# Both long-convolution filters beside the up panels, start-up loads in another order, and modulation panels summed four to a bank

## The chip, the cores and the metric

One core of a Trainium2 chip runs the whole program. The metric is the device time of one execution in microseconds (us). The kernel before took 2073.51 us (median of 3 runs, 2073.36 to 2076.2).

## What is computed

One transformer block of a first model and two layers of a second, for 256 tokens of width 1024, in float32. What matters here is how the first block begins:

```
h  = x + grid_pos_embed(256);  hc = ctx
m  = split(silu(c)     @ mod_w + mod_b, 9)      # 9 vectors of 1024, for the tokens
mc = split(silu(c_ctx) @ mod_w + mod_b, 9)      # and 9 for the context
h  = half_ffn(h,  m[0],  m[1],  m[2],  w_gate, w_up, w_down)
hc = half_ffn(hc, mc[0], mc[1], mc[2], w_gate, w_up, w_down)
...                                             # later: modulate(rms_norm(h), m[3], m[4]) and so on
hyena_kernels(256, w1, b1, freq1, w2, b2, freq2, w3)   # two filters ("orders") for a long convolution
```

`half_ffn` takes the RMS norm of its input, scales and shifts it by the first two vectors, multiplies by the gate and up weights (1024 x 2816 each), applies silu, and multiplies by the down weight. The filters come from a small network with two sine layers on position features. They need nothing of x, and are used only much later, in the mixer.

## The kernel before, in words

**Weights.** Every large weight is cut into panels of 128 x 2048 float32 (1 MB). SyncE (SP) issues their loads in order into a ring of four slots, `landing` (L519, L527). GpSimd (POOL) rounds a panel to its high part `whi` (`high`, L569 and L570), VectorE (DVE) subtracts it to get the low part `wlo` (`low`, L643), and TensorE (PE) makes each product of three matmuls: high x high, high x low, low x high (`product`, L1830 to L1832). A panel of the up stage is 48 matmuls with 512 columns, tokens and context side by side.

**Modulation.** The first 8 panels of the stream (`lead`) hold mod_w for the first two of the nine vectors, which the norm of the first half_ffn needs. The other 28 (`rest`) are worked beside the 22 up panels and come through two more slots in `ws` (`load_rest`, L536). One panel is 8 matmuls with `cst`, silu of c and c_ctx, as a stationary of 32 columns, whose first two count (`mod_product`, L1956); the results lie in four groups of 32 partitions. ScalarE (ACT) copies the bank to `mrow` (`mod_copy`, L1512), PE sums the four groups and turns the row into columns with two matmuls against the 0/1 matrix `fold` (`turn`, L1987), and after each four panels DVE adds the bias into `mcol` (`add_mod`, L792). So there are 36 copies, 36 turns and 9 additions.

**Filters.** `filter_layer` (PE, L1997), `sine_argument` (DVE, L745 to L750) and `sine` (ACT, L1502) give the features `h2`. Per order, `taps` (PE, L2010) makes the taps in two halves, `windowed` (DVE, L757) multiplies by the window, `fold_kernel` (L762 to L765) adds and subtracts the two directions, `absolute` (L773 to L775) and `tap_sums` (PE, L2020) give the L1 norm, `inverse_norm` (L779, L781) its reciprocal, `spectrum` (PE, L2034 and L2038) the Fourier transform in four parts, `normed_spectrum` (L788) scales it, and `spill` (ACT, L1498) stores it to HBM.

**The order of the work** is written out by hand, one program per engine, with semaphores between them; each engine runs its list in order, so a wait holds up all behind it. PE's start is: lead 0, lead 1, filter_layer 0, turn 0, lead 2, turn 1, filter_layer 1, lead 3, turn 2, lead 4, turn 3, taps(0, 0), lead 5, turn 4, taps(0, 1), the sums of squares of the tokens (`norm_sum`, L1925), lead 6, turn 5, the sums of squares of the context, lead 7, turns 6 and 7. Then come the 22 up panels, with tap_sums(0) behind panel 0, spectrum(0) behind 1, the taps of order 1 behind 2 and 3, tap_sums(1) behind 5 and spectrum(1) behind 6. From panel 7 on, one rest panel is worked in the middle of an up panel and one behind it, each with the turn of an earlier one but for the first two; two turns stand in the middle of the last up panel.

ACT begins with 14 DMA issues (L1475 to L1489), then makes silu(c) (L1493, semaphore `c_silu`), on which all of PE waits. DVE begins with the two sine arguments, adds the position embedding to h (L805), waits for the window and the folded transform matrix (`hw_in`, two loads), does windowed(0, 0), windowed(0, 1) and fold_kernel(0), then add_mod(0) and add_mod(1), the gains (L816), and the norm: for each of eight chunks k two multiplications (L822), ACT's addition of the shift (L1538) and two subtractions (L828). `low` of the first up panel stands behind the step k == 1.

Of the kernel before, what the change touches and what calls it, by code (L numbers as in the profile page):

```python
# [20 lines left out]
ALU = mybir.AluOpType  # L21
# [49 lines left out]
REST_FROM = 7  # L71
# [15 lines left out]
def columns(*sizes):  # L87
    out, at = {}, 0
    for name, n in sizes:
# [11 lines left out]
                      ("rot_ret", P), ("fold", 2))  # L101
# [6 lines left out]
def shape_constants():  # L108
# [5 lines left out]
    mats["fold"][p % 32 == 0, 0] = 1  # L114
    mats["fold"][p % 32 == 1, 1] = 1
# [111 lines left out]
def build(nc, stream, xT, ctxT, vec1, vec2, lbrow, hyw, mats, tabs, masks, posemb, hyc, window, zT, spectra, out):  # L227
    with ExitStack() as ctx:
# [19 lines left out]
        cst = sb("cst", [P, KD, 32])  # L248
# [49 lines left out]
        mrow = W(2048, UNROLL, COLS)  # L298
# [27 lines left out]
        flb = sb("flb", [P, 4])  # L326
# [90 lines left out]
        flb_in, h3w_in, hw_in = sem("flb_in"), sem("h3w_in"), sem("hw_in")  # L417
        def turn_bank(i):
            return 5 if i == 1 else 4
# [96 lines left out]
        def _(sp):  # L516
            sp.dma_start(v1[:], vec1).then_inc(vec_in, 16)
            for g in range(SLOTS):
                sp.dma_start(landing[:, g], stream[g]).then_inc(landed[g], 16)  # L519
# [17 lines left out]

            for g in range(SLOTS, N_LEAD + REST_FROM + SLOTS):
# [5 lines left out]
            follow = N_LEAD + REST_FROM + SLOTS + N_REST // 2  # L544
# [79 lines left out]
        def _(dve):  # L624
# [127 lines left out]
            def windowed(o, u):  # L752
                dve.wait_ge(h3_mm, 2 * o + u + 1)
                if o and u == 0:
                    dve.wait_ge(kf_mm, 4)
                for d in range(2):
                    last = v.tensor_tensor(kern[:, d, u * 512:(u + 1) * 512], ps[:, 6 + d], hwindow[:, d, u], ALU.mult)  # L757
                last.then_inc(win_mul, 1)
# [31 lines left out]
            def add_mod(i):  # L790
                dve.wait_ge(mod_turned, i * UNROLL + UNROLL)
                v.tensor_tensor(mcol[:, i * 8:i * 8 + 8, :],  # L792
                                ps[:, turn_bank(i), 0:16].rearrange("p (c b) -> p c b", b=2),
                                m1("mod_b", 0, 72)[:, i * 8:i * 8 + 8].unsqueeze(2).to_broadcast([P, 8, 2]), ALU.add
                                ).then_inc(mod_added, 1)
# [3 lines left out]
            sine_argument(1)  # L799
# [19 lines left out]
            for k in range(KD + 1):  # L819
# [11 lines left out]
                if k == 1:  # L831
                    low(G_UP1, G_UP1 % SLOTS)

            def beside_up1(i):
                if i == 0:
                    absolute(0)
                if i == 5:
                    absolute(1)
                if i == 1:
                    inverse_norm(0)  # L840
                if i == 2:
                    normed_spectrum(0, 0)
                    normed_spectrum(0, 1)
                if i == 3:
                    normed_spectrum(0, 2)
                    normed_spectrum(0, 3)
                    windowed(1, 0)
                if i == 4:
                    windowed(1, 1)
                    fold_kernel(1)  # L850
                if i == 6:
                    inverse_norm(1)
                if i == 7:
                    normed_spectrum(1, 0)
                    normed_spectrum(1, 1)
                if i == 8:
                    normed_spectrum(1, 2)
                    normed_spectrum(1, 3)
                q = i - REST_FROM - 3
                if q >= 0 and q % 2 == 0:  # L860
# [1655 lines left out]
```

## Time and profile before

| | |
|---|---|
| median of 3 runs | 2073.51 us |
| the profiled execution | 2071.93 us, its span 2069.9 us |
| PE busy | 1932.9 us (93%) |
| DVE, POOL, ACT busy | 1147.3, 601.3, 383.9 us |
| granted TensorE clock, mean | 0.976 |
| moved by DMA | 307.83 MB, mean 149 GB/s |

Times in the trace count from the span's start. A row of the timeline gives start, duration, engine, line, what is written and read, how many instructions were merged, and in brackets how long the engine stood idle before and what released it. PE is the matmul, PEld its weight load; ACTq and SPq are DMA issues of ScalarE and SyncE. The granted clock is 1.0 at 2.4 GHz and 0.5 at 1.2 GHz. Each float32 matmul leaves more than one record, so a modulation panel of 8 matmuls is "x16" and a turn of 2 is "x4".

### The profile page before, as it was taken

The numbers are of one execution on the slowest core, as the hardware profiler recorded it, in microseconds if no ns is written. First come the engines' busy times: TensorE is split into PE (matmuls) and PEld (weight loads), VectorE is DVE, ScalarE is ACT, GpSimd is POOL, SyncE is SP. The second block draws the span as 40 slices with busy tenths as digits, with TensorE's granted clock in tenths as the row PEclk, the third lists the DMA queues.
The fourth block names the chain that finished last, engine by engine and source line by source line (L and its number), as shares of the span: only waits on it lengthen the run. The fifth ranks groups of instructions, "written<-read, shape, count | busy, mean of one in ns | idle before, by whom it ended". The sixth has DMA issues, their size and how long they took to land.

```text
span 2069.9 us, 33025 instructions
## 1 busy us (share of the span) xinstructions
PE 1932.9 (93%) x13818; PEld 1758.2 (85%) x13818; DVE 1147.3 (55%) x1219; ACT 383.9 (19%) x718; POOL 601.3 (29%) x505
## 2 busy tenths in 40 slices
PE   4899999999997878899989999889999999889999
PEld 2576777887997867799989997789999999689999
DVE  3652221325258976644575776675556676576554
ACT  1200000113122230211122122411112102432110
POOL 0111111121235611233333332133334333123333
PEclk8899999999999989999999999999999999999999
DMA  8336655321233212355544443235554434134552
GB/s 311 113 108 218 237 210 201 131 102 61 103 127 128 95 69 102 112 188 183 181 152 166 143 143 122 102 126 184 182 183 175 151 140 156 69 141 165 183 183 102
DMA packets 44913, 307.83 MB, mean 149 GB/s; under 512 B 5376, under 2 KB 5888, under 8 KB 8320
## 3 DMA queue, kind: packets, MB, share of 16 engines
q1 hardware_dynamic: 40752, 292.66, 39.8%
q10 hardware_dynamic: 4048, 13.49, 1.8%
q8 instruction: 93, 1.52, 0.3%
q14 instruction: 20, 0.16, 0.0%
HBM read 302.98 MB, written 3.15 MB: 148 GB/s over the span
## 4 chain that ended last, share of the span: by engine, by line
PE 78%; DVE 12%; issue 4%; POOL 2%; ACT 2%; DMA 2%; ACTq 0%; DVEq 0%; POOLq 0%
PE ps L1830 23%; PE ps L1831 22%; PE ps L1832 22%; DVE wlo L643 3%; POOL whi L570 2%; DMA ws<-in_hyc 2%; PE ps L1956 1%; PE ps L2312 1%; PE ps L1925 1%; PE ps L2219 1%; PE ps L2336 1%; DVE xlo L703 1%; PE ps L1987 1%; PE ps L2179 1%; PE ps L2289 1%
## 5 line engine op out<-in xcount | busy, mean ns | idle before, releaser
L1830 PE MATMUL ps<-xhi,whi 128*128 128x256 f32 (+1 forms) x3680 | 1121.0, 305 | 37.5 <-DVE xlo L651 21.4
L1831 PE MATMUL ps<-xlo,whi 128*128 128x256 f32 (+1 forms) x3680 | 1104.1, 300 | 0.0
L1832 PE MATMUL ps<-xhi,wlo 128*128 128x256 f32 (+1 forms) x3680 | 1103.6, 300 | 0.0
L643 DVE TENSOR_TENSOR wlo<-landing,whi 128x2048 fp32r<-128x2048 f32 x242 | 562.3, 2323 | 460.0 <-POOL whi L570 459.3
L1830 PEld LDWEIGHTS ps<-xhi,whi 128*128 128x128 f32 x3680 | 710.1, 193 | 74.2 <-issue 31.1
L1831 PEld LDWEIGHTS ps<-xlo,whi 128*128 128x128 f32 x3680 | 710.3, 193 | 22.8 <-issue 2.2
L1832 PEld LDWEIGHTS ps<-xhi,wlo 128*128 128x128 f32 x3680 | 709.6, 193 | 21.2
L569 POOL TENSOR_TENSOR whi<-landing,ones 128x128 fp32r<-128x128 f32 x242 | 124.4, 514 | 1445.1 <-PE ps L1832 1404.2
L570 POOL TENSOR_SCALAR whi<-landing 128x1920 fp32r<-128x1920 f32 x242 | 442.9, 1830 | 0.0
L881 DVE TENSOR_TENSOR big<-big,ps 128x512 f32<-128x512 f32 x22 | 15.1, 687 | 184.7 <-ACT big L1555 184.7
L1467 ACT ACTIVATE xhi<-big 128x512 fp32r (+3 forms) x66 | 45.9, 696 | 385.7 <-PE ps L1832 331.2
L1830 PE MATMUL ps<-whi,xhi 128*128 128x256 f32 (+1 forms) x288 | 84.9, 295 | 10.4 <-DVE wlo L643 4.0
L1831 PE MATMUL ps<-wlo,xhi 128*128 128x256 f32 (+1 forms) x288 | 82.4, 286 | 0.0
L1832 PE MATMUL ps<-whi,xlo 128*128 128x256 f32 (+1 forms) x288 | 82.2, 285 | 0.0
L651 DVE TENSOR_TENSOR xlo<-big,xhi 128x512 fp32r<-128x512 f32 (+1 forms) x82 | 62.0, 756 | 13.9 <-ACT xhi L1777 13.7
L1830 PEld LDWEIGHTS ps<-whi,xhi 128*128 128x128 f32 x288 | 56.4, 196 | 13.4 <-DVE wlo L643 5.0
L1831 PEld LDWEIGHTS ps<-wlo,xhi 128*128 128x128 f32 x288 | 56.5, 196 | 0.0
L1832 PEld LDWEIGHTS ps<-whi,xlo 128*128 128x128 f32 x288 | 56.4, 196 | 0.0
L1196 DVE TENSOR_REDUCE smx<-ps 128x2 f32<-128x512 f32 x32 | 22.1, 690 | 52.2 <-PE ps L2312 52.2
L1731 ACT ACTIVATE ws<-ps,smx 128x256 f32<-128x256 f32 x64 | 29.7, 470 | 110.4 <-DVE smx L1198 110.4
L2179 PE MATMUL ps<-ws 128*128 128x128 f32 x224 | 30.8, 298 | 16.2 <-DVE ws L978 16.1
L1809 ACT ACTIVATE big<-ws 128x512 f32 (+1 forms) x32 | 20.2, 632 | 137.7 <-DVE ws L1329 137.7
(269 smaller groups left out, 1379.3 us busy)
## 6 DMA issues: line engine op xcount, KB each, us to landing
landing<-in_stream SPq DMA_DIRECT2D x250, 1024.0 KB, 4.8
ws<-in_stream SPq DMA_DIRECT2D x28, 1024.0 KB, 4.8
spectra<-big ACTq DMA_DIRECT2D x8, 256.0 KB, 6.1
ws<-spectra ACTq DMA_DIRECT2D x2, 1024.0 KB, 4.9
ws<-in_tabs ACTq DMA_DIRECT2D x1, 1280.0 KB, 5.5
h<-in_xT ACTq DMA_DIRECT2D x1, 1024.0 KB, 15.7
ws<-in_window ACTq DMA_DIRECT2D x1, 1024.0 KB, 23.7
ws<-in_ctxT ACTq DMA_DIRECT2D x1, 1024.0 KB, 28.2
```

Of the source, the lines that this page charges most:

```text
L569: pool.tensor_tensor(hi[:, 0:P], panel[:, 0:P], ones[:], ALU.mult)
L570: pool.tensor_scalar(hi[:, P:n], panel[:, P:n], 1.0, 0.0, ALU.mult, ALU.add).then_inc(hi_done, 1)
L643: v.tensor_tensor(wlo[:, s % 2], landing[:, s], whi[:, s % 2].bitcast(F32), ALU.subtract).then_inc(lo_done, 1)
L651: v.tensor_tensor(alo[:, r_phase % 2, :, 0:t], src, ahi[:, r_phase % 2, :, 0:t].bitcast(F32), ALU.subtract).then_inc(act_lo, 1)
L703: v.scalar_tensor_tensor(xlo[:, k, 0:T], h[:, k], gain(k), xhi[:, k, 0:T].bitcast(F32), ALU.mult, ALU.subtract).then_inc(norm_lo, 1)
L1196: lstep(v.tensor_reduce(st[:, 0:2], ps[:, 2 + 2 * (n % 2):4 + 2 * (n % 2), 0:T], AX, ALU.max, negate=True))
L1467: a.activation(ahi[:, j, :, 0:t], src(i + skip), ACT.Identity).then_inc(act_hi, 1)
L1731: last = a.activation(ew[n % 2][:, m], ps[:, 2 + 2 * (n % 2) + m, 0:T], ACT.Exp, bias=st[:, 2 + m:3 + m], scale=0.125, accum_out=st[:, 4 + ...
L1830: mm(out, w_hi, x_hi, start=first, stop=False, skip_group_check=True)
L1831: mm(out, w_hi, x_lo, start=False, stop=False, skip_group_check=True)
L1832: return mm(out, w_lo, x_hi, start=False, stop=last, skip_group_check=True)
L2179: last = mm(ps[:, b + u, o], e[:, x], e[:, x], start=True, stop=True)
```

## The change

Five edits.

1. ACT's first loads: mats, x, the position embedding, the two halves of hyw, zT; then silu(c); then ctx, the window, and the two parts of hw3. The folded transform matrix (with a semaphore of its own) and v2all are issued behind sine(1). The two small loads of `flb` go to SP, between v1 and the first panel.
2. `cst` becomes 6 columns wider, with silu(c) at columns 6 and 7. The stationary of panel j of a group of four starts at column 6 - 2j, so the panel's results land on rows 2j and 2j + 1 of each group of 32 partitions, and four panels add up in one bank. One copy and one turn with 8 columns then do four panels: 9 copies and 9 turns in all.
3. Taps, window and fold of order 0 leave the start. Order o now has both halves of the taps behind panel 4o, window and fold on DVE at 4o + 1, the absolute values at 4o + 2 with tap_sums and three spectrum parts behind that panel, the norm and two scaled parts at 4o + 3 with the last spectrum part behind it, and the other two scaled parts at 4o + 4.
4. The rest panels start behind up panel 7 rather than in the middle of it; the last one stands in the middle of the last up panel, and the last turn behind the seventh of its eight chunks.
5. PE's start: lead 0, 1, filter_layer 0, lead 2, 3, filter_layer 1, lead 4, turn 0, lead 5, tokens' squares, lead 6, context's squares, lead 7, turn 1. DVE adds the embedding before the second sine argument. ACT: sine(0), squares of tokens, sine(1), two loads, squares of context, mod_copy(0), the table load, both roots, mod_copy(1). `low` of the first up panel stands behind k == 2.

```diff
-REST_FROM = 7
+REST_FROM = 8
...
@@ sync
             sp.dma_start(v1[:], vec1).then_inc(vec_in, 16)
+            for d in range(2):
+                sp.dma_start(flb[64 * d:64 * d + 64], vec1[0:64, VEC1["b1"][0]:VEC1["b1"][0] + 4]).then_inc(flb_in, 16)
             for g in range(SLOTS):
                 sp.dma_start(landing[:, g], stream[g]).then_inc(landed[g], 16)
...
-            for i in range(N_REST // 2):
-                load(N_LEAD + REST_FROM + SLOTS + i, (N_LEAD + REST_FROM + SLOTS + i) % SLOTS)
-                load_rest(2 * i)
-                load_rest(2 * i + 1)
+            first_rest = N_LEAD + REST_FROM + SLOTS
+            for g in range(SLOTS, first_rest):
                 load(g, g % SLOTS)
+                if g == first_rest - 2:
+                    load_rest(0)
+            load_rest(1)
+            for i in range(N_REST // 2 - 1):
+                load(first_rest + i, (first_rest + i) % SLOTS)
+                load_rest(2 * i + 2)
+                load_rest(2 * i + 3)
@@ vector
             sine_argument(0)
-            sine_argument(1)
             dve.wait_ge(x_in, 32)
...
-            dve.wait_ge(h_set, 4)
-            dve.wait_ge(hw_in, 32)
-            windowed(0, 0)
-            windowed(0, 1)
-            fold_kernel(0)
+            sine_argument(1)
             add_mod(0)
             add_mod(1)
...
-                if k == 1:
+                if k == 2:
                     low(G_UP1, G_UP1 % SLOTS)
 
             def beside_up1(i):
...
+                o, t = divmod(i, 4)
+                if o < 2 and t == 1:
+                    windowed(o, 0)
+                    windowed(o, 1)
+                    fold_kernel(o)
+                if o < 2 and t == 2:
+                    absolute(o)
+                if o < 2 and t == 3:
+                    inverse_norm(o)
+                    normed_spectrum(o, 0)
+                    normed_spectrum(o, 1)
+                if o in (1, 2) and t == 0:
+                    normed_spectrum(o - 1, 2)
+                    normed_spectrum(o - 1, 3)
+                if i in MOD_TURN:
+                    add_mod(LEAD_GROUPS + MOD_TURN.index(i))
@@ scalar
+            act.dma_start(mat[:], mats).then_inc(small_in, 16)
+            act.dma_start(h[:].rearrange("p k t -> p (k t)"), xT).then_inc(x_in, 16)
+            act.dma_start(ws[:, FILT + 3968:FILT + 3968 + POS], posemb).then_inc(x_in, 16)
             act.dma_start(hyin[0:64, 0:128], hyw[:, 0:128]).then_inc(hy_in, 16)
             act.dma_start(hyin[64:128, 0:128], hyw[:, 0:128]).then_inc(hy_in, 16)
             act.dma_start(zfeat, zT).then_inc(hy_in, 16)
...
+            a.activation(cst[:, :, C_AT:C_AT + 2], m1("c", 0, 2 * KD).rearrange("p (k b) -> p k b", b=2), ACT.Silu
+                         ).then_inc(c_silu, 1)
+            act.dma_start(ws[:, 0:2048], ctxT).then_inc(ctx_in, 16)
+            act.dma_start(hwindow.rearrange("p d u c -> p (d u c)"), window).then_inc(hw_in, 16)
...
+            sine(1)
+            act.dma_start(fdft, hyc[:, 1024:1792]).then_inc(dft_folded_in, 16)
+            act.dma_start(v2all[:], vec2.rearrange("l p n -> p l n")).then_inc(v2all_in, 16)
             act.wait_ge(ctx_in, 16)
             for b in range(4):
                 squares(1, hc, b)
-            mod_copy(7)
+            mod_copy(0)
             log_exp()
             norm_rms(0, 2)
             norm_rms(1, 3)
+            mod_copy(1)
@@ tensor
+            def mod_product(n, panel):
+                i, j = divmod(n, UNROLL)
+                at_ = C_AT - 2 * j
                 for k in range(KD):
                     q = 32 * (k % 4)
-                    last = mm(out[q:q + 32], cst[:, k], panel[:, k * COLS:(k + 1) * COLS], start=k < 4, stop=k >= 4,
+                    last = mm(ps[q:q + 32, mod_bank(i), 0:COLS], cst[:, k, at_:at_ + 32], panel[:, k * COLS:(k + 1) * COLS],
+                              start=j == 0 and k < 4, stop=j == UNROLL - 1 and k >= 4, skip_group_check=True)
...
             lead(0)
             lead(1)
             filter_layer(0)
+            lead(2)
+            lead(3)
+            filter_layer(1)
+            lead(4)
             turn(0)
...
-                elif 0 <= j < N_REST:
+                elif i >= REST_FROM:
                     feature_panel(s, up_out(i), 0, 2 * T, (0,))
                     rest(j)
-                    if j:
-                        turn(N_LEAD + j - 2)
                     last = feature_panel(s, up_out(i), 0, 2 * T, (1,))
...
+                if i >= REST_FROM - 1 and j + 1 < N_REST - 1:
                     rest(j + 1)
-                    if j:
-                        turn(N_LEAD + j - 1)
+                if i in MOD_COPY[:-1]:
+                    turn(LEAD_GROUPS + MOD_COPY.index(i))
+                o, t = divmod(i, 4)
+                if o < 2 and t == 0:
+                    taps(o, 0)
+                    taps(o, 1)
+                if o < 2 and t == 2:
+                    tap_sums(o)
+                    spectrum(o, (0, 1, 2))
+                if o < 2 and t == 3:
+                    spectrum(o, (3,))
```

`MOD_COPY` is 9, 11, ..., 21 and `MOD_TURN` 10, 12, ..., 20, 21: ACT copies a group in the second half of an odd up panel, PE turns it behind that panel, and DVE adds it in the next even one. `load_rest(0)` still waits for window (1, 1), `load_rest(1)` for the last spectrum part of order 1, and the later ones for the rest panel two before.

## Rows read from the trace of the kernel before

**Rows 1.** Busy time, share of the DMA engines and GB/s of one stretch:

```profile
core 0: us, PE busy (x) PEld busy (x) DVE busy (x) ACT busy (x) POOL busy (x), PEclk, DMA share, GB/s
30.00:40.00 10.00, 0.00 (x0) 0.00 (x0) 0.56 (x1) 0.00 (x0) 0.00 (x0) 0.57 1.02 418
```

**Rows 2.** The chain that ended last, start-up (start us, us, what):

```profile
8.23 31.13 DMA ws<-in_hyc
```

**Rows 3.** Timeline of the start, DMA issues of ScalarE:

```profile
2.00 0.60 ACTq L1477 DMA_DIRECT2D big<-in_zT  x1
6.72 0.45 ACTq L1485 DMA_DIRECT2D ws<-in_posemb  x1
7.69 0.51 ACTq L1487 DMA_DIRECT2D ws<-in_ctxT  x1
8.72 2.52 ACTq L1489 DMA_DIRECT2D v2all<-in_vec  x1
```

**Rows 4.** DMA issues by line: KB each, us from issue to landing:

```profile
ws<-in_ctxT ACTq DMA_DIRECT2D x1, 1024.0 KB, 28.2
...
ws<-in_posemb ACTq DMA_DIRECT2D x1, 136.0 KB, 17.9
big<-in_zT ACTq DMA_DIRECT2D x1, 128.0 KB, 8.3
```

**Rows 5.** Timeline of the start, compute of 12 to 29 us:

```profile
12.89 3.64 PE L1956 MATMUL ps<-landing,cst 128*32 128x256 f32 x32 [12.89 <-ACT cst L1493]
...
16.46 1.12 PE L1997 MATMUL ps<-big,ws 64*64 64x256 f32 x4
...
17.69 0.55 DVE L745 TENSOR_SCALAR big<-ps,flb 128x256 f32<-128x256 f32 x1 [16.24 <-PE ps L1997]
...
20.63 0.42 ACT L1502 ACTIVATE ws<-big 128x256 f32<-128x256 f32 x1 [3.65 <-DVE big L750]
...
25.09 2.77 DVE L805 TENSOR_TENSOR h<-h,ws 128x256 f32<-128x256 f32 x8
...
26.18 2.34 ACT L1386 ACTIVATE big<-h 128x512 f32<-128x512 f32 x4
```

**Rows 6.** Timeline, from the sums of squares to the norm:

```profile
42.79 4.78 PE L1925 MATMUL ps<-big,ones 128*128 128x256 f32 x16
...
49.59 3.72 PE L1925 MATMUL ps<-big,ones 128*128 128x256 f32 x16 [0.48 <-ACT big L1386]
...
53.24 1.07 PE L1956 MATMUL ps<-landing,cst 128*32 128x256 f32 x16
...
55.67 0.25 DVE L816 TENSOR_SCALAR gains<-mcol 128x8 f32<-128x8 f32 x2
...
57.93 0.48 DVE L822 SCALAR_TENSOR_TENSOR big<-h,gains,rstd 128x256 f32<-128x256 f32 x1 [2.01 <-ACT rstd L1382]
```

**Rows 7.** The chain, one step of the norm:

```profile
63.38 0.79 DVE xlo L828 x2
```

**Rows 8.** Timeline, the first up matmul and the first tap sums:

```profile
62.65 0.80 PE L1830 MATMUL ps<-xhi,whi 128*128 128x512 f32 x1 [7.22 <-DVE wlo L643]
...
78.94 3.66 PE L2020 MATMUL ps<-ws,ones 128*128 128x512 f32 x4 [2.22 <-DVE ws L775]
```

**Rows 9.** The chain, filter work between the up panels:

```profile
110.28 1.06 PE ps L2010 x4
...
145.53 1.72 PE ps L2020 x4
```

**Rows 10.** The chain, three rest panels in turn:

```profile
176.20 1.00 PE ps L1956 x16
...
182.90 1.00 PE ps L1956 x16
...
190.03 1.00 PE ps L1956 x16
```

**Rows 11.** Timeline of DVE in up panel 5, the end of the absolute values:

```profile
141.71 1.22 DVE L775 SCALAR_TENSOR_TENSOR ws<-ws,big 128x1024 f32<-128x1024 f32 x1
```

**Rows 12.** Line of the rest loads, all 28, us to landing:

```profile
DMA to landing us min/median/max: 4.7/4.8/8.7
```

More of the change, by code:

```diff
@@ L70 @@
 PANELS = G_LAYER + LAYERS * PER_LAYER
-REST_FROM = 7
+REST_FROM = 8
+N_GROUP, LEAD_GROUPS = N_MOD // UNROLL, N_LEAD // UNROLL
+C_AT = 2 * (UNROLL - 1)
 DVE_LINKS, ACT_LINKS = 65, 6
@@ L113, in shape_constants @@
     mats["ident"][:] = np.eye(P)
-    mats["fold"][p % 32 == 0, 0] = 1
-    mats["fold"][p % 32 == 1, 1] = 1
+    for r in range(2 * UNROLL):
+        mats["fold"][p % 32 == r, r] = 1
     mats["block64"][:] = (p[:, None] // 64 == p[None] // 64)
@@ L325, in build @@
         ang = chunks(33, 2)
-        flb = sb("flb", [P, 4])
+        flb = scol[:, 0:4]
         KF_BANK = (6, 7, 4, 5)
@@ L753, in windowed @@
                 dve.wait_ge(h3_mm, 2 * o + u + 1)
+                if o == 0 and u == 0:
+                    dve.wait_ge(hw_in, 16)
                 if o and u == 0:
@@ L1893, in last_panel @@
                         beside()
+                    if k == KD - 2:
+                        behind()
                 return last
@@ L2004, in taps @@
                 elif u == 0:
-                    pe.wait_ge(kf_done, 2)
-                else:
-                    pe.wait_ge(win_mul, 2 * o + 1)
+                    pe.wait_ge(kf_done, 4)
+                if o == 0 and u == 1:
+                    pe.wait_ge(mod_added, 3)
                 for d in range(2):
                     r = slice(64 * d, 64 * d + 64)
-                    last = mm(ps[:, 6 + d], h2[r, u * P:(u + 1) * P], hw3[r, o * 512:(o + 1) * 512], start=True, stop=True)
+                    last = mm(ps[:, KF_BANK[2 * u + d]], h2[r, u * P:(u + 1) * P], hw3[r, o * 512:(o + 1) * 512], start=True, stop=True)
                 last.then_inc(h3_mm, 1)
@@ L2021, in tap_sums, with spectrum @@
                 last.then_inc(l1_mm, 1)
-            def spectrum(o):
-                for m in range(4):
+            def spectrum(o, ms):
+                for m in ms:
                     if m == 0:
-                        pe.wait_ge(win_mul, 2 * o + 2)
-                        pe.wait_ge(mod_added, 3)
+                        pe.wait_ge(folded_k, o + 1)
+                        if o == 0:
+                            pe.wait_ge(dft_folded_in, 16)
                     if m == 3:
@@ L2043, in _ @@
             filter_layer(0)
+            lead(2)
+            lead(3)
+            filter_layer(1)
+            lead(4)
             turn(0)
-            lead(2)
-            turn(1)
-            filter_layer(1)
-            lead(3)
-            turn(2)
-            lead(4)
-            turn(3)
-            taps(0, 0)
             lead(5)
-            turn(4)
-            taps(0, 1)
             pe.wait_ge(const_set, 3)
@@ L2059, in _ @@
             lead(6)
-            turn(5)
             for b in range(4):
@@ L2063, in _ @@
             lead(7)
-            turn(6)
-            turn(7)
+            turn(1)
             def up_out(i):
```

179 lines of the change are left out of this document (58 added, 121 removed).

## The prediction

> **What bounds the kernel now.** I read the busy table by stretches first. After the start-up TensorE is busy nearly all the time and everything it does adds to the time, so a gain has to come from PE work left out of the up stage, or from a first up matmul that starts earlier. Before that the table shows a hole: from 30 to 40 us PE does nothing, while the DMA engines are full, moving 418 GB/s [rows 1]. The chain of waits names what the hole waits for: the folded transform matrix, issued at 8.23 and there 31.13 us later, at 39.4 [rows 2]. DVE waits for it before it windows the taps of order 0, PE waits for DVE before the second half of those taps, and the sums of squares, leads 6 and 7 and the norm stand behind in PE's list. The timeline gives the rest: PE's first matmul at 12.89, released by silu(c), which stands behind 14 DMA issues of ACT; the first filter layer at 16.46, though its last load, zT, was there at 2.00 + 8.3 = 10.3 [rows 3 to 5]; the norm's first multiplication at 57.93; the first up matmul at 62.65 [rows 6, 8]. In the up stage I read the chain of waits for the spacing of like work.
>
> **Up stage: turns.** A rest panel without a turn is 182.90 - 176.20 = 6.70 us from the next, with one 190.03 - 182.90 = 7.13 [rows 10]; a turn costs 0.43 on PE, which is the bound there. Of 28 turns 7 stay: 21 x 0.43 = 9.0 us saved. The four panels summed in a bank cost what they did: the same matmuls with the same 32 columns. A turn with 8 columns instead of 2 moves six columns more in each of two matmuls; I take it at the same 0.43. ACT's copy leaves nothing on the path: it stands half an up panel before its turn. The last one, behind four of the last panel's eight chunks, has two chunks and more before its turn.
>
> **Up stage: filters.** Today tap_sums(0) is waited for by 2.22 us and takes 3.66, where the same work in the full-clock stretch takes 1.72 without a wait [rows 8, 9]: 2.22 + 3.66 - 1.72 = 4.2 saved, since DVE now has all of panel 2 for the absolute values. Against that both halves of the taps of order 0 come in, 2 x 1.06 = 2.1 [rows 9]. Spectra and order 1 are the same work at other places. Do they wait? In today's panel 5 DVE ends the absolute values at 141.71 + 1.22 = 142.9 and PE asks for them at 145.53 [rows 9, 11]: 2.6 us of slack, in the very pattern that both orders now get. Window and fold in one panel are one pair of multiplications more than today in a panel that has two taps before it; I take nothing. Net of the filters: 4.2 - 2.1 = 2.1.
>
> **Up stage: queues.** On SP, load_rest(1) now waits for the last spectrum part of order 1, and a panel load and load_rest(2) queue behind it. It lands 4.7 to 8.7 us after its issue [rows 12], and PE wants it after half a panel, 6.70 less the rest product's 1.00 and its edges, about 5.5 [rows 10]. So nothing at the median, at most 3.2 once. The loads behind it are wanted some panels later. Every later rest load has a whole period of 13.6 (2 x 6.70 and, every second time, a turn) less one rest product, 12.4: no wait at 8.7.
>
> **Start-up, up to the first filter layer.** silu(c) comes behind six issues instead of 14, so leads 0 and 1 run as their panels land; the two small flb loads hold up SP's first panel by about 1.3 us (two issues like zT's 0.60), which the next wait hides. That wait is zT. It now stands behind mats, x (1024 KB) and the embedding (136 KB), in a queue that shares full DMA engines with SP's panels. Lower bound by bytes: mats, x and embedding are 1.61 MB, at 418 GB/s 3.9 us, so 10.3 + 3.9 = 14.2. Upper bound: the embedding's landing today, 6.72 + 17.9 = 24.6 [rows 3, 4], behind all that will be ahead of zT and the two parts of hw3 besides. I take 19.0: the upper bound less two more small transfers, at 2.8 each as a guess inside the bounds. The layer takes 1.2 (16.46 to 17.69) [rows 5], so DVE starts at 20.3 rather than 17.69.
>
> The Trainium skill speaks against this part: "DMA: Bandwidth & Descriptors", section Queues, rings and completion order, says that each DMA engine takes packets in turn from the queues that have work, so a small transfer behind others pays for its place rather than its size. The trace agrees: zT, 128 KB, took 8.3 us [rows 4]. By this rule as an estimate each of the three transfers put ahead drags a 1 MB panel along, which gives zT at about 21.5, and the sum below would be 2.5 us worse.
>
> **Start-up, from there to the norm.** PE has turn(0) ahead of lead 5, and turn(0) waits for a copy that ACT makes behind the squares of the context. So the path is: sine argument 2.94 (17.69 to 20.63), additions 2.77, second sine argument 2.94, sine 0.42 [rows 5]; two DMA issues, 0.5 and 2.52 as v2all's today [rows 3]; squares 2.34 [rows 5]; copy and turn 1.2 (the 2.68 from 53.24 to 55.92 less lead 7's 1.07, the gains' 0.25 and the short bias addition); lead 5, 1.5 between 1.07 and twice that, since PE has stood idle and its clock is low then (0.57 granted in the hole); token sums 4.78, lead 6 1.07, context sums 3.72, and from lead 7 to the gains 2.68 less a turn, 2.25 [rows 1, 6]. The roots and their table load are now hidden behind lead 7. That is 28.9, with 0.8 for a dozen handovers 29.7. The norm starts at 20.3 + 29.7 = 50.0, so 7.9 earlier. The context, at 35.9 today (7.69 + 28.2) [rows 3, 4], has less ahead of it and should land near 25, before ACT asks at 32.
>
> **Low behind k == 2.** One norm step is two multiplications and two subtractions, 2 x 0.79 = 1.6 [rows 7]. The first up matmul comes 1.6 later in the norm, and PE, not DVE, sets the pace of panel 0 today, so 1.6 is lost. It would cost less if DVE's steps set that pace.
>
> **Sum.** 9.0 + 2.1 + 7.9 - 1.6 = 17.4 us. The profiled execution took 2071.93 (span 2069.9), so its like would be 2054.5; the median of the runs stands 1.6 above it, at 2073.51, and gives 2056.1.
>
> **Rivals.**
> (a) The filter's loads are early: zT by the lower bound, 14.2, and v2all's issue costs 0.5 (today it is the last of a full row of issues). The norm starts at 15.5 + 27.7 = 43.2, 14.7 earlier; in all 9.0 + 2.1 + 14.7 - 1.6 = 24.2, so 2049.3. For it: 128 KB is little. Against: rows 4.
> (b) The start-up gives nothing back: the one turn that gates five PE items, a cold clock through both sums, zT at 24.6, and the norm starts at 56 to 58. Then the up stage alone counts: 9.0 + 2.1 - 1.6 = 9.5 and up to 2 more, 2062 to 2064. For it: every small load waits its turn today. Against: the 10 us hole has no successor in the new lists.
> (c) The turn saves less than 0.43, say because eight columns cost, or DVE is late at window and fold: half of 9.0 gone, 2060.6.
> (d) Slower: the rest loads set the pace. Each of two slots goes load, product, load; a period of 13.6 leaves 12.4 for a load. At 17.9 us, which the embedding took when the DMA engines were full [rows 4], 13 periods would be 5.5 longer each, 72 in all: 2128. It decides from a landing of 13.7 (13 x 1.3 = 17). Against: none of 28 took over 8.7 [rows 12], and the order of loads is nearly today's.
> (e) That four panels in a bank are not one copy and one turn: the lists say so plainly, and no wait undoes it.
>
> **Chances.** The forecast 0.55, (a) 0.20, (b) 0.13, (c) 0.08, (d) 0.02, and 0.02 for a disturbance that I do not see. The likeliest is 2056.1. From (a) and (b) I take the range 2049.5 to 2063.5: it drops the outer half of (a) and the end of (b), and (d). A measurement of this kernel tells 0.2%, 4.1 us, from no change: faster by over that 0.94, within it 0.03, slower 0.03.
>
> **What would show it.** PE's first matmul near 8; the first filter layer between 15 and 24, and right at 19; a wait of turn(0) for ACT's copy, with leads and sums close behind it; the norm near 50, the first up matmul 6.3 behind it. Panel 0 runs into the taps without a wait. Spacing of rest panels 6.70, with a turn every fourth, 7 turns behind the lead groups. From the end of panel 0 to the last up matmul 11 us less than today. It is wrong if the norm starts after 56, if PE waits at a tap_sums or at rest 1, or if the copy stands on the path in the up stage.

## The result, and the profile after

The changed kernel took 2049.73 us (median of 4 runs, 2048.82 to 2050.41) where the kernel before took 2073.51 (4 runs, 2073.36 to 2076.2): a ratio of 0.9883 [0.9868, 0.9899], 24 us less. The forecast was 2056.1, so the kernel came out 6.4 us below the forecast, at the lower end of its range (2049.5 to 2063.5). The profiled executions (2071.93 and 2049.11) stand 1.6 and 0.6 us below their medians, and their spans differ by 2069.9 - 2047.1 = 22.8 us. I divide up these 22.8; the forecast of the same quantity was 17.4.

The busy table by stretches, same columns as [rows 1]; the fourth column group is DVE, the last two numbers are the DMA engines' share and GB/s:

```profile
30.00:40.00 10.00, 8.34 (x53) 5.58 (x54) 0.17 (x1) 3.78 (x7) 0.00 (x0) 0.70 1.02 395
...
52.49:56.40 3.91, 3.91 (x9) 3.13 (x10) 3.91 (x11) 2.19 (x5) 0.00 (x0) 0.50 0.75 245
...
65.47:351.62 286.15, 286.15 (x1540) 208.04 (x1540) 96.83 (x84) 16.22 (x29) 46.84 (x42) 1.00 0.51 191
```

The hole of [rows 1] is gone: 8.34 of 10 us busy. The last line is the up stage from the end of panel 0 to the last up matmul: PE is busy for all of its 286.15 us, at a granted clock of 1.00, so none of the new waits stands on the path there. The same stretch of the kernel before:

```profile
62.65:68.80 6.15, 6.15 (x15) 4.80 (x16) 6.15 (x16) 3.63 (x8) 0.00 (x0) 0.50 0.51 173
...
76.72:374.56 297.84, 295.62 (x1617) 217.22 (x1616) 88.95 (x75) 24.32 (x50) 48.09 (x42) 0.99 0.53 183
```

The 22.8 us come from three places, each bounded by the same two events in both kernels:

| stretch | before | after | less | forecast |
|---|---|---|---|---|
| start to the norm's first multiplication | 57.93 | 46.19 | 11.7 | 7.9 |
| from there to the first up matmul | 4.72 | 6.30 | -1.6 | -1.6 |
| panel 0, first matmul to the last | 14.07 | 12.98 | 1.1 | 0 |
| end of panel 0 to the last up matmul | 297.84 | 286.15 | 11.7 | 11.1 |
| the rest of the span | 1695.3 | 1695.5 | -0.2 | 0 |

So two thirds of the 5.4 us by which the forecast of the span fell short lie in the start-up. This is its chain of waits (start, length, what), to be set against [rows 2, 5, 6]:

```profile
4.37 17.89 DMA landing<-in_stream
22.31 1.93 PE ps L1947 x16
...
25.34 0.55 DVE big L760
...
28.28 0.34 ACT ws L1498
28.66 0.45 ACTq L1514
29.15 2.19 ACT big L1386 x4
...
31.66 1.02 PE ps L1978 x4
32.68 1.87 PE ps L1947 x16
34.55 4.35 PE ps L1914 x16
38.89 1.00 PE ps L1947 x16
39.89 3.65 PE ps L1914 x16
43.55 1.04 PE ps L1947 x16
...
46.19 1.67 DVE big L835 x4
```

Its long wait is the landing of a panel, for lead 3 at 22.31 (L1947 is lead, L1988 filter_layer, L1914 the sums of squares, L1978 turn). Nothing in it is the folded matrix, and nothing is zT. The timeline shows how zT dropped out:

```profile
3.50 0.64 ACTq L1480 DMA_DIRECT2D big<-in_zT  x1
...
10.88 1.93 PE L1947 MATMUL ps<-landing,cst 128*32 128x256 f32 x16 [10.88 <-DMA landing<-in_stream]
...
15.31 1.11 PE L1988 MATMUL ps<-big,ws 64*64 64x256 f32 x4
...
22.31 1.93 PE L1947 MATMUL ps<-landing,cst 128*32 128x256 f32 x16 [3.03 <-DMA landing<-in_stream]
```

silu(c) now ends at 5.7, yet PE's first matmul waits for its panel until 10.88 (forecast near 8); lead 1 waits likewise, and the first filter layer comes right behind lead 1 without a wait. zT had landed at 3.50 + 11.3 = 14.8.

In the up stage the spacing of rest panels is as [rows 10]: 6.70 without a turn and 7.13 with one, now only every fourth time.

```profile
181.19 1.00 PE ps L1947 x16
...
187.90 1.00 PE ps L1947 x16
188.90 0.54 PE ps L1978 x4
...
195.03 1.00 PE ps L1947 x16
```

The taps and the tap sums, which the forecast priced from [rows 9]:

```profile
65.47 1.92 PE ps L2001 x8
...
89.37 1.72 PE ps L2008 x4
...
118.78 1.92 PE ps L2001 x8
```

Both halves of the taps took 1.92 instead of 2 x 1.06, in order 1 (118.78) as in order 0, and the tap sums 1.72 without a wait, as forecast.

### The profile page after: what moved, and what is told of

The parts are those of the page before. It is cut to its first block, busy times and chain, and to the rows that moved or that the text cites. A ratio compares the mean times of both kernels' runs of the same rounds, so it can differ in the third digit from the quotient of the medians.

```text
span 2047.1 us, 32753 instructions
## 1 busy us (share of the span) xinstructions
PE 1918.0 (94%) x13710; PEld 1744.7 (85%) x13710; DVE 1146.0 (56%) x1219; ACT 374.5 (18%) x691; POOL 600.6 (29%) x505
## 4 chain that ended last, share of the span: by engine, by line
PE 80%; DVE 11%; issue 4%; POOL 2%; ACT 2%; DMA 1%; SPq 0%; ACTq 0%; DVEq 0%; POOLq 0%
PE ps L1817 24%; PE ps L1818 23%; PE ps L1819 23%; DVE wlo L658 2%; POOL whi L585 2%; PE ps L1947 2%; PE ps L2290 1%; DMA landing<-in_stream 1%; PE ps L2197 1%; PE ps L1914 1%; PE ps L2314 1%; DVE xlo L718 1%; PE ps L2157 1%; PE ps L2267 1%; DVE ws L978 1%
## 5 line engine op out<-in xcount | busy, mean ns | idle before, releaser
L1818 PEld LDWEIGHTS ps<-xlo,whi 128*128 128x128 f32 x3680 | 710.1, 193 | 21.7 <-issue 1.4
L1817 PE MATMUL ps<-whi,xhi 128*128 128x256 f32 (+1 forms) x288 | 84.9, 295 | 10.5 <-DVE wlo L658 4.0
L1544 ACT ACTIVATE big<-ps 128x512 f32<-128x512 f32 x22 | 13.2, 598 | 224.1 <-PE ps L1819 224.1
```

The costliest lines, as they stand in the source:

```text
L1817: mm(out, w_hi, x_hi, start=first, stop=False, skip_group_check=True)
L1818: mm(out, w_hi, x_lo, start=False, stop=False, skip_group_check=True)
```

## The experiments

Twelve kernels ran in three batches, each beside the kernel before. Ratios are to that kernel in the same batch, with a 95% interval; the medians of before were 2073.19, 2071.92 and 2071.42 us.

| kernel | batch | median us | ratio |
|---|---|---|---|
| a_low_k1 | 1 | 2047.43 | 0.9874 [0.9853, 0.9895] |
| b_filter1_early | 1 | 2050.78 | 0.9889 [0.9867, 0.9911] |
| c_turn0_late | 1 | 2049.56 | 0.9880 [0.9859, 0.9902] |
| d_combined | 1 | 2047.78 | 0.9875 [0.9857, 0.9893] |
| e_spare_turns | 2 | 2060.43 | 0.9938 [0.9922, 0.9955] |
| f_before_fdft_apart | 2 | 2063.51 | 0.9959 [0.9946, 0.9971] |
| g_filter_loads_first | 2 | 2048.79 | 0.9881 [0.9863, 0.9899] |
| h_v2all_in_burst | 2 | 2048.60 | 0.9886 [0.9868, 0.9904] |
| i_flb_on_act | 3 | 2051.78 | 0.9897 [0.9874, 0.9921] |
| j_high_after_low | 3 | 2049.23 | 0.9883 [0.9866, 0.9900] |
| k_window_late | 3 | 2043.58 | 0.9852 [0.9833, 0.9871] |
| l_window_late_high | 3 | 2043.15 | 0.9856 [0.9838, 0.9874] |

The changed kernel ran four times; i ran twice, d five times, f seven and the others four. The intervals are 5 to 10 us wide, so differences of 1 to 3 us are read from the traces, by the times of like events.

### The turns: e_spare_turns

The 21 turns that the change removes are put back as spare ones, behind rest panels, with nothing that waits for them.

```diff
+            def spare_turn():
+                for c in range(2):
+                    mm(ps[:, 5, 8 * c:8 * c + 8], mat[:, c * P:(c + 1) * P], mat[:, MATS["fold"][0]:MATS["fold"][0] + 2 * UNROLL], start=True, stop=True)
...
                     rest(j)
+                    if i >= REST_FROM + 2:
+                        spare_turn()
...
                     rest(j + 1)
+                if i >= REST_FROM + 2 and i < N_UP - 1 and i != N_UP - 2 - 0:
+                    spare_turn()
```

> The changed kernel with 21 spare turns in the up stage, each two matmuls of 8 columns into a bank that nobody reads then, behind 21 of the rest panels. Theory A (a turn costs PE what the chain showed): 21 x 0.43 = 9.0 us longer. Rival B (turns were partly hidden, or the gain in the up stage was another's): 4 us or less.

2060.43 us, 10.7 above the changed kernel's median; the ratios leave room for 5 to 18. The trace is sharper: the last up matmul ends at 361.06 instead of 351.62, of which 0.3 is the start-up (panel 0 ends at 65.79 instead of 65.47). 9.1 for 21 is 0.43 each. Between 188.22 and 347.16 every rest panel now stands 7.13 from the next, or 7.57 where a spare turn and one of the kernel's own stand between them:

```profile
202.46 1.00 PE ps L1947 x16
203.46 0.54 PE ps L1983 x4
...
209.59 1.00 PE ps L1947 x16
```

The term of 9.0 is confirmed: a turn costs its place in PE's list and no more.

### The hole: f_before_fdft_apart

The kernel before, with one edit: DVE's wait for the window no longer includes the folded transform matrix, and PE asks for that matrix at the first spectrum part.

```diff
-            act.dma_start(fdft, hyc[:, 1024:1792]).then_inc(hw_in, 16)
+            act.dma_start(fdft, hyc[:, 1024:1792]).then_inc(dft_folded_in, 16)
...
-            dve.wait_ge(hw_in, 32)
+            dve.wait_ge(hw_in, 16)
...
+                        if o == 0:
+                            pe.wait_ge(dft_folded_in, 16)
                         pe.wait_ge(win_mul, 2 * o + 2)
```

> The kernel before, where the folded transform matrix has a semaphore of its own, asked for at the first spectrum; windowing waits for the window alone. Theory A (the hole from 30 to 40 us is the wait for that matrix): the wait ends with the window at 30.9, then the context's squares at 35.9 are next, and the norm starts near 50 rather than 57.93: 7 to 9 us shorter than before, so that half of the change's start-up gain needs no reordering of work. Rival B (the bytes of the start-up bound it): the hole stays until the lead panels have landed, under 3 us.

2063.51 us, 8.4 less than before by the medians. The stretch of the hole, and DVE's windowing:

```profile
30.00:40.00 10.00, 9.51 (x64) 6.04 (x57) 6.40 (x9) 2.29 (x6) 0.00 (x0) 1.00 1.02 415
```
```profile
30.26 1.29 DVE L758 TENSOR_TENSOR ws<-ps,ws 128x512 f32<-128x512 f32 x2 [2.32 <-DMA ws<-in_window]
```

PE is busy for 9.51 of 10 us at full clock, with no order of work changed. The norm starts at 47.39 (expected near 50), 10.5 earlier than in the kernel before; the whole change brought 11.7. So one wait, which named a load that its work did not need, was nearly all of what the change won in the start-up. With that wait gone, the other new orders of the start-up add 1.2 us between them. The last up matmul ends 9.3 earlier (365.23 against 374.56): 1.2 of the 10.5 are lost again on the way. They are lost at the first tap sums, which start 17.75 us behind the first up matmul, where the kernel before has 16.29. The last of the absolute values meets POOL's rounding and takes 2.69, where the same step took 1.36 before:

```profile
65.97 2.76 POOL L571 TENSOR_SCALAR whi<-landing 128x1920 fp32r<-128x1920 f32 x1
67.12 2.69 DVE L776 SCALAR_TENSOR_TENSOR ws<-ws,big 128x1024 f32<-128x1024 f32 x1
```

### Is zT the wait? g_filter_loads_first

The filter's loads go ahead of mats, x and the embedding on ACT's queue, and leave their place behind them.

```diff
+            act.dma_start(hyin[0:64, 0:128], hyw[:, 0:128]).then_inc(hy_in, 16)
+            act.dma_start(hyin[64:128, 0:128], hyw[:, 0:128]).then_inc(hy_in, 16)
+            act.dma_start(zfeat, zT).then_inc(hy_in, 16)
             act.dma_start(mat[:], mats).then_inc(small_in, 16)
             act.dma_start(h[:].rearrange("p k t -> p (k t)"), xT).then_inc(x_in, 16)
             act.dma_start(ws[:, FILT + 3968:FILT + 3968 + POS], posemb).then_inc(x_in, 16)
```

> The changed kernel with hyw and zT ahead of mats, x and the embedding, as before the change. Theory A (lead 3's panel, not zT, holds the second filter layer): the first filter layer can start some 7 us earlier and the norm does not move by more than 1 us. Rival B (zT's place sets the start, the prediction's step): the norm starts 3 us or more earlier.

```profile
big<-in_zT ACTq DMA_DIRECT2D x1, 128.0 KB, 3.0
```

zT lands 3.0 us after its issue, nearly 10 us earlier in the run than in the changed kernel (5.0 against 14.8), and the first filter layer starts at 15.00 instead of 15.31; the norm starts at 46.56, not earlier. That layer waits in PE's list behind lead 1, and lead 1 for its panel, and lead 3 still waits 3.1 us for its own panel. The new order of the loads did move something: lead 3 starts at 20.98 instead of 22.31, and the second sine argument 1.3 earlier (24.01). The 1.3 are lost again in the token sums, which took 5.42 instead of 4.35 as the clock rose later, and in the gains (L829), 0.85 instead of 0.24 beside POOL's rounding. So g shows that zT is not the wait; it does not show that the order of ACT's first loads is worth nothing.

### What the path is made of: b_filter1_early and c_turn0_late

```diff
@@ b_filter1_early
             lead(2)
-            lead(3)
             filter_layer(1)
+            lead(3)
             lead(4)
@@ c_turn0_late
             lead(4)
-            turn(0)
             lead(5)
...
             lead(7)
+            turn(0)
             turn(1)
```

> The changed kernel with PE's second filter layer ahead of lead 3. Theory A (the start's path goes from the landing of panel 3 through lead 3 to the second filter layer, the second sine, the context's squares, the copy and turn 0): the second sine argument starts near 22.2 rather than 25.34, and the norm starts up to 3 us earlier, as far as lead 4's panel, there at 27.0, lets turn 0 go. Rival B (the landings of the lead panels set the norm's start): the sine moves and the norm stays at 46.2.

> The changed kernel with turn 0 taken from ahead of lead 5 to behind lead 7. Theory A (turn 0's wait for ACT's copy holds up lead 5 and both sums): the 3.6 us wait and the 1.0 of the turn leave the path, lead 5 starts near 28.2, and the norm starts 3.5 to 4.5 earlier, at 42 to 43. Rival B (lead panels' landings): lead 5 waits for its panel instead and the norm gains under 1.5. If the first up panel's high part, ready at 43.5, becomes the bound, low waits for it and the first matmul gains less than the norm.

Chain of b, then of c:

```profile
15.44 16.06 DMA landing<-in_stream
...
31.54 1.93 PE ps L1947 x16
33.48 5.21 PE ps L1914 x16
```
```profile
15.22 15.66 DMA landing<-in_stream
...
30.93 1.94 PE ps L1947 x16
32.86 5.65 PE ps L1914 x16
```

In b the second sine argument starts 3.0 earlier (22.31 against 25.34), in c PE no longer waits for the copy, and in both lead 5 moves up (31.54 and 30.93 against 32.68) and then waits for its panel. The norm starts at 45.98 and 46.03 against 46.19, as rival B of both had it. The wait behind the copy is the panel's landing, and it limits what the order of PE's list can bring to the 1.1 and 1.8 us by which lead 5 moved.

The token sums (L1914, the same 16 matmuls) took 5.21 and 5.65 here and 4.35 in the changed kernel, so they took back 0.9 and 1.3 of that. Over the ten kernels whose sums stand at this place (the changed one, a to e, g to j) they took 4.15 to 5.75, the clock rising at another point of them each time. That is 1.6 us of noise on this path, as large as what b and c moved.

### Low of the first up panel: a_low_k1

```diff
-                if k == 2:
+                if k == 1:
                     low(G_UP1, G_UP1 % SLOTS)
```

> The changed kernel with low of the first up panel back behind k == 1. Theory A (PE sets the pace of up panel 0): the first up matmul comes one norm step, 1.6 us, earlier, at about 50.9 rather than 52.49, and the end of panel 0 with it, so the whole run is 1.6 us shorter. Rival B (DVE's norm steps set the pace of panel 0): the first matmul is 1.6 earlier and the end of the panel stays at 65.5; no gain.

The norm starts 0.3 earlier than in the changed kernel (45.87), the first up matmul 1.9 earlier (50.59), so 1.6 of it belong to the edit, and panel 0 ends 1.2 earlier (64.24), 0.9 of it the edit's. Panel 0 took 13.65 us here and 12.98 there, and the low clock accounts for the 0.7 between them: PE was at it for 5.2 us here and 3.9 there.

```profile
50.59:55.80 5.21, 5.21 (x12) 4.12 (x13) 5.21 (x14) 2.81 (x7) 0.00 (x0) 0.50 0.55 201
```

The stretch varied as much between kernels that do the same there (see panel 0 in the next part). Without the difference the 1.6 arrive at the end of the panel too, so PE sets its pace, and rival B is out.

The median is 2.3 below the changed kernel's; their ratios' intervals overlap, so the whole-program effect is not shown.

### All small steps together: d_combined, and POOL: j_high_after_low

d is a, b and c together, with the folded matrix and v2all issued behind the table load. j is d with POOL held:

```diff
@@ d_combined, beside a, b and c
-            act.dma_start(fdft, hyc[:, 1024:1792]).then_inc(dft_folded_in, 16)
-            act.dma_start(v2all[:], vec2.rearrange("l p n -> p l n")).then_inc(v2all_in, 16)
...
             mod_copy(0)
             log_exp()
+            act.dma_start(fdft, hyc[:, 1024:1792]).then_inc(dft_folded_in, 16)
+            act.dma_start(v2all[:], vec2.rearrange("l p n -> p l n")).then_inc(v2all_in, 16)
@@ j_high_after_low, in the loop of high
+                if isinstance(g, int) and g == N_LEAD + 1:
+                    pool.wait_ge(lo_done, 1)
```

> Low behind k == 1, second filter layer ahead of lead 3, turn 0 behind lead 7, and the two late loads issued by ACT behind the table load for the roots. Theory A: the norm near 40 to 42, the first up matmul 4.7 behind it but not before the high part at 43.5 plus 2.3 for low, so near 46 to 47 against 52.49; the run 5 to 6 us shorter than the changed kernel, near 2044. Rival B (landings): under 2 us.

> Run d with POOL's high part of the second up panel held until low of the first is done. Theory A (in run d the norm's first multiplication took 1.89 rather than 0.48 us because POOL was at work beside it, and this cost the gain): it takes 0.48, the first up matmul comes 1.4 us earlier than d's 50.40, and the end of panel 0 with it if PE sets its pace. Rival B (a DVE operation is held up by POOL wherever it falls): the 1.4 us come back in a later step, and the end of panel 0 stays at 63.4.

d: 2047.78, no better than a alone, where 5 to 6 us below the changed kernel were expected; it is the rival, the landings. Lead 5 waits for its panel until 30.79; the norm starts at 44.27, 1.9 earlier, but its first step then runs beside POOL's rounding of the second up panel:

```profile
44.10 1.79 POOL L585 TENSOR_SCALAR whi<-landing 128x1920 fp32r<-128x1920 f32 x1
44.27 1.89 DVE L835 SCALAR_TENSOR_TENSOR big<-h,gains,rstd 128x256 f32<-128x256 f32 x1
46.09 0.47 DVE L835 SCALAR_TENSOR_TENSOR big<-ws,gains,rstd 128x256 f32<-128x256 f32 x1
```

The same operation takes 1.89 beside POOL and 0.47 when POOL is done. The Trainium skill ("SBUF — State Buffer", Who interferes with whom) says that a DVE instruction with two SBUF inputs contends with a GpSimd instruction that reads SBUF, and that the shared ports are an exclusive lock; these rows agree: DVE's step ends 0.27 us after POOL's. j moves POOL's rounding behind the low part, and the stretch moves with it, into panel 0:

```profile
51.43 1.97 POOL L587 TENSOR_SCALAR whi<-landing 128x1920 fp32r<-128x1920 f32 x1
51.66 2.40 DVE L843 SCALAR_TENSOR_TENSOR xlo<-big,mcol,xhi 128x256 fp32r<-128x256 f32 x2
```

The two subtractions take 2.40 there, where 0.87 is usual. j is 2049.23 us; its norm starts 1.8 later than d's, and 1.4 of that are the token sums (5.64 against 4.22). The collision can be moved but was not avoided.

### The price of a DMA issue: h_v2all_in_burst and i_flb_on_act

The forecast took v2all's issue at 2.52 as in [rows 3]; it takes 0.45 in the changed kernel (28.66 in the chain above). h puts both late loads back at the end of ACT's first burst, 12 issues in all; i also moves the two small flb loads from SP to ACT, 14 in all, as many as the kernel before has.

```diff
@@ h: behind the two parts of hw3
+            act.dma_start(fdft, hyc[:, 1024:1792]).then_inc(dft_folded_in, 16)
+            act.dma_start(v2all[:], vec2.rearrange("l p n -> p l n")).then_inc(v2all_in, 16)
@@ i: h, and behind zT
             for d in range(2):
-                sp.dma_start(flb[64 * d:64 * d + 64], ...).then_inc(flb_in, 16)
+                act.dma_start(flb[64 * d:64 * d + 64], ...).then_inc(flb_in, 16)
```

> The changed kernel with the folded transform matrix and v2all issued at the end of ACT's first burst rather than behind the second sine. Theory A (an issue costs more when many loads are under way): v2all's issue takes over 2 us again as before the change, but off the path, and the 0.8 us of both issues leaves the path behind the second sine, so the norm is about 0.8 earlier, less what 0.4 MB more ahead of the lead panels costs. Rival B (v2all's issue has one price, 0.45): it takes 0.45 there too.

> The kernel of run h (both late loads at the end of ACT's first burst) with the two flb loads back on ACT, behind zT, so that ACT issues 14 loads in one burst as before the change. Theory A (the long issue comes with the number of loads outstanding on one queue): v2all's issue takes 2 us or more again, where run h showed 0.45 with 12. Rival B (it came from something else, such as which data the DMA engines move then): 0.45 to 0.7.

The last issue of h, then of i:

```profile
7.64 0.45 ACTq L1492 DMA_DIRECT2D v2all<-in_vec  x1
```
```profile
8.98 2.30 ACTq L1492 DMA_DIRECT2D v2all<-in_vec  x1
```

The same load costs 0.45 as the 12th issue of a burst and 2.30 as the 14th (2.52 in the kernel before, 2.00 in f). So rival (a)'s price, 0.5 "as the last of a full row of issues", was the right reading of [rows 3]. Whether the count of loads, their amount or something else makes the price stays open; in l the same issue took 1.24, as the fifth of a late burst. In h ACT's squares of the context start 0.45 earlier behind the second sine and the norm 0.3 earlier (45.91).

i costs elsewhere too: the flb loads now land late, at 4.92 + 16.77 = 21.7, and the first sine argument waits for them until 21.82; the norm starts at 48.99. Its first panel is there 1.0 earlier (lead 0 starts at 9.87, not 10.88), since SP issues it from 1.18 on, without the flb loads ahead.

### The landings themselves: k_window_late and l_window_late_high

If the panels' landings are the path, other loads should leave the queues. k is d with the window and hw3 (three loads, 1.5 MB), which are first wanted in up panel 0 and later, issued behind the table load and no longer behind ctx; l is k with j's wait on POOL.

```diff
@@ scalar, beside d
             mod_copy(0)
             log_exp()
+            act.dma_start(hwindow.rearrange("p d u c -> p (d u c)"), window).then_inc(hw_in, 16)
+            for d in range(2):
+                taps = hyw[:, 128:2176].rearrange("p (o d c) -> p d o c", d=2, c=512)
+                act.dma_start(hw3[64 * d:64 * d + 64].rearrange("p (o c) -> p o c", c=512), taps[:, d]).then_inc(h3w_in, 16)
             act.dma_start(fdft, hyc[:, 1024:1792]).then_inc(dft_folded_in, 16)
```

> Run d with the window and hw3 (1.5 MB, wanted behind panel 0) issued with the two late loads, behind the table load for the roots. Theory A (the landings of the lead panels are the bound that runs b to d met): 1.5 MB at 0.42 MB per us leave up to 3.7 us; panel 5, there at 30.8 in d, lands near 28, the first up panels near 38 rather than 41.2, and the norm starts 2 to 3.5 earlier, near 41 to 42. Rival B (PE's own list from lead 5 on, 13 us, is the bound): under 1 us.

> Run k with POOL's high part of the second up panel held until low of the first is done, the best guess for a faster version: as k, since both high parts are then done before the norm begins; about 2043.5 if theory A of k holds, 2046 if not.

```profile
22.80 12.52 DMA landing<-in_stream
35.36 1.07 PE ps L1947 x16
...
38.07 1.67 DVE big L835 x4
39.74 2.52 DVE xlo L841 x2
...
44.46 2.52 DVE big L835 x2
```

k: the norm starts at 38.07, 8.1 earlier than in the changed kernel and 6.2 earlier than in d, where 2 to 3.5 were expected. Lead 5 starts at 25.78, 6.8 earlier than in the changed kernel. From there on PE is nearly without a wait: 0.21 us ahead of lead 7, though the chain names that panel's landing. The two sums of squares take 3.72 each; the token sums gain 0.6 by that, the granted clock being up before they begin. PE's waits for panels ahead of them are under one microsecond each; whether that is why the clock was up was not tested. Of the 8.1 us, 6.7 arrive: panel 0 ends at 58.78, the last up matmul at 344.94. POOL works against it, as its roundings now fall into the norm: two pairs of DVE's steps take 2.52 where 0.79 is usual, 3.5 us in all, and PE stops for want of xlo at 47.4.

k took 2043.58 us (2040.06 to 2044.53), l 2043.15 (2041.11 to 2044.46): about 6 below the changed kernel, 1.5% below the kernel before. No run of either overlaps one of the changed kernel's four, though the intervals of the ratios do by a hair (0.9871 and 0.9868). In l lead 5 waits for its panel until 25.82, the norm starts at 39.33 and its first four steps take 3.07 instead of 1.67; l is not distinguishable from k. These are the best versions that ran.

## Why the prediction was right or wrong

**What bounds the kernel: right.** The hole and its cause were named from [rows 1, 2], and f shows that cause alone: 10.5 us.

**The turns, 9.0: right,** shown by e (9.1) and by the spacing of 6.70 and 7.13. **The filters, 2.1: right in kind,** 2.7 from the stage's 11.7 less 9.0. The forecast left out what surrounds the taps. Behind each stop for taps PE's first product takes 0.43 instead of 0.23, so order 0's taps cost 1.92 + 0.2, the forecast's 2.1. Order 1's stood behind two panels before, twice 1.06 + 0.2, and stand behind one now, 1.92 + 0.2: 0.4 of the excess of 0.6. **The queues, 0: right;** PE has no idle time in the stage, and the rests stood where the list puts them. **Low behind k == 2, 1.6:** right at the first up matmul (6.30 behind the norm, as forecast); a shows 1.6 there and, with the clock's 0.7 taken out, at the end of panel 0 too.

**The start-up, 7.9: 11.7 measured.** This is the step that failed. Its mechanism was right from the second sine argument on and wrong ahead of it, and two sentences of it fail.

"That wait is zT" is false. The path from the start to the second sine argument runs through the landing of lead 3's panel (chain of the changed kernel), and in g, with zT there at 5.0, lead 3 still waits for its panel and the norm is no earlier. The forecast listed zT's landing, then DVE's work, and never asked when the panels of leads 1 to 3, which stand around the filter layers in PE's list, would be there. By luck the two paths are of like length: 26.0 forecast for the second sine argument, 25.34 measured. The range for zT, 14.2 to 24.6, did hold the 14.8; the guess of 19.0 inside it had no row behind it. With zT falls what was to hide behind it: the two flb loads on SP, 1.3, were put at nothing because "the next wait hides" them. They stand in the chain of panels, and i, which has them elsewhere, has its first panel 1.0 earlier; what that is worth at the norm no run shows, as i's norm waits for the flb loads themselves.

"Two DMA issues, 0.5 and 2.52 as v2all's today" is the larger error. From the second sine argument to the norm the forecast counted 24.0 (26.0 to 50.0), and the trace has 20.85 (25.34 to 46.19):

| item | forecast | measured |
|---|---|---|
| second sine argument | 2.94 | 2.94 |
| sine and two DMA issues | 3.44 | 0.87 |
| squares of the context | 2.34 | 2.10 |
| copy and turn | 1.2 | 1.36 |
| lead 5, token sums, lead 6, context sums | 11.07 | 10.87 |
| lead 7 to the norm | 2.25 | 2.71 |
| handovers, counted by themselves | 0.8 | in the rows above |

2.6 of the 3.2 are the issues: each took 0.34 to 0.45, and the first one lay beside the sine. In [rows 3] v2all's 2.52 stands at the end of a burst whose other rows show 0.45 to 0.60; behind a pause of 20 us the ordinary price was the one to take. h and i show the same issue cheap at the end of 12 and dear at the end of 14. The handovers were in good part counted twice, since durations taken from start to start contain them. From lead 7 to the norm it took 0.46 more than forecast: PE now waits 0.50 for ACT's copy ahead of turn 1, a time in which the kernel before worked turn 6, so taking out that turn saved nothing there.

**Panel 0, nothing forecast, 1.1 measured.** Before, PE had the granted clock of 0.50, the lower of the two levels (1.2 GHz), for 6.15 us of panel 0, after it for 3.9; half of the difference is the 1.1. It can't be put down to the change. The low stretch was this long in the kernels with the same work in panel 0 (us):

| kernel | h | f | changed | d | e | g | b | c | a | i | before |
|---|---|---|---|---|---|---|---|---|---|---|---|
| PE idle ahead of panel 0 | 7.31 | 7.23 | 6.83 | 6.68 | 6.83 | 7.44 | 6.83 | 7.07 | 5.27 | 6.83 | 7.22 |
| low clock in panel 0 | 3.2 | 3.5 | 3.9 | 3.9 | 4.1 | 4.3 | 4.8 | 5.0 | 5.2 | 5.3 | 6.15 |

f has the kernel before's order of work, stood idle as long, and had 3.5. With the same 6.83 of idle time it was 3.9 to 5.3. So the forecast could not have had a term of a fixed size here; what sets the length stays open. The Trainium skill ("TensorE: Matmul & The Clock Gate", Part 1) says that the cold stretch of one kernel varies from run to run; these rows, of one run of each kernel, are in keeping with that.

**The Trainium skill's rule about packets taken in turn** ("DMA: Bandwidth & Descriptors", Queues, rings and completion order) gave zT at 21.5 by my estimate, a megabyte of panels for each transfer put ahead. Measured: 14.8, so that estimate was far too dear. What does hold is that the other queue matters. In the kernel before and in g, zT is ACT's third load and is issued at 2.00 in both; before, SP's first panels are issued from 1.18 on and zT takes 8.3 us, in g they are issued from 2.42 on and it takes 3.0. The rule is in keeping with that; the amount per turn was my addition.

**The rivals.** (a), 2049.3, is where the time came out, but only its price of v2all's issue and its zT (14.2 for 14.8) held; it had the norm at 43.2, and the panels kept it at 46.2, while panel 0, the up stage and the median's distance from the profiled execution gave 1.1, 0.6 and 1.0 that it did not count. That its sum came out is luck. (b) is excluded by the norm at 46.19, (c) by e and by the stretch without idle time, (d) by the stretch without idle time, (e) by the 7 turns in the up stage.

## What to carry to other kernels

When a start-up is full of loads, list for each item of the in-order engine which load it needs and when that lands, and work out the path from the latest of them: here one wait for a load that its work did not need cost 10 us (f), and loads issued long before they were wanted cost another 6 at the norm's start (k against d). Moving compute in such a list gains little until the loads themselves are put in the order of need (b and c brought 0.2 us at the norm). A duration at the end of a row of issues is not the price of an issue elsewhere, and a path whose terms are taken from start to start has its handovers in it already.

## What I had not expected of the hardware

- The same DMA issue on ACT took 0.45 us as the 12th of a burst and 2.30 as the 14th; 2.00 to 2.52 in three kernels with 14.
- A load of 128 KB, third on its queue and issued at the same time, took 8.3 us with panels of the other queue issued 0.8 us ahead of it and 3.0 with them 0.4 us behind it.
- Two DVE steps of 0.47 us became 1.89 and, in k, 2.00 beside a rounding on POOL. It goes the other way too; in k POOL's small step waits out DVE's long one, 2.01 where 0.46 is usual:

```profile
42.19 2.28 DVE L658 TENSOR_TENSOR wlo<-landing,whi 128x2048 fp32r<-128x2048 f32 x1
42.77 2.01 POOL L584 TENSOR_TENSOR whi<-landing,ones 128x128 fp32r<-128x128 f32 x1 [0.77 <-DMA landing<-in_stream]
```

- The low clock at the start of panel 0 lasted 3.9, 4.1, 4.8 and 5.3 us in four kernels that had all stood idle for 6.83 us ahead of it, and 3.5 and 6.15 after 7.23 and 7.22 us.
